# Up-projections with 512 moving columns: the low and high halves of the activations in one matmul, added at the eviction

## What is computed

```python
# gated net (four of them, ffn0 to ffn3), hidden width 2816
y = (silu(h @ w_gate) * (h @ w_up)) @ w_down
# net with a convolution (two of them, ffn4 and ffn5)
def conv_ffn(h, w_up, cw, cb, w_down):
    gu = causal_dwconv(h @ w_up, cw, cb)
    g, u = jnp.split(gu, 2, axis=-1)
    return (jax.nn.gelu(g, approximate=True) * u) @ w_down
```

## Time and profile before

| what | value |
|---|---|
| median of 3 runs | 1914.26 us (1911.96 to 1915.06) |
| the profiled execution's own time | 1912.59 us |
| its span | 1910.8 us |
| mean granted TensorE clock | 0.982 |
| PE busy | 1820.1 us (95%) in 11714 matmuls |
| DVE busy | 1409.9 us (74%) in 2264 instructions |
| ACT busy | 950.9 us (50%) in 1382 instructions |
| read from HBM | 379.90 MB, 199 GB/s over the span |

### The profile page before, as it was taken

How to read it: one execution, slowest core, us unless ns; L and a number is a source line. 1 busy time by engine, 2 the same in 40 slices (tenths; PEclk the granted TensorE clock), 3 DMA queues, 4 the chain that set the end, 5 groups by cost and what they waited for, 6 DMA issues and landing times.

```text
span 1910.8 us, 31883 instructions
## 1 busy us (share of the span) xinstructions
PE 1820.1 (95%) x11714; PEld 1619.5 (85%) x11714; DVE 1409.9 (74%) x2264; ACT 950.9 (50%) x1382; POOL 129.5 (7%) x170
## 2 busy tenths in 40 slices
PE   6999899899999999999999999999889998979998
PEld 5998677699989997788878799978689987769996
DVE  7778888687778778868665565558778866877884
ACT  5444465454435443555454454445664435664443
POOL 1001010000010000000000000000012200002210
PEclk9999999899999999999999999999999999999999
DMA  9878666357788777455530255554254554324453
GB/s 384 339 272 312 231 234 214 126 212 275 279 290 297 267 278 269 163 176 177 191 137 1 82 224 184 189 183 181 70 194 179 177 197 154 111 88 176 176 186 122
DMA packets 63782, 382.11 MB, mean 200 GB/s; under 512 B 7153, under 2 KB 7409, under 8 KB 27586
## 3 DMA queue, kind: packets, MB, share of 16 engines
q1 hardware_dynamic: 42912, 300.96, 43.8%
q0 software_dynamic: 20208, 78.79, 11.4%
q10 hardware_dynamic: 578, 1.22, 0.2%
HBM read 379.90 MB, written 1.05 MB: 199 GB/s over the span
## 4 chain that ended last, share of the span: by engine, by line
PE 86%; DVE 7%; ACT 4%; issue 1%; DMA 1%; SPq 1%; DVEq 0%; ACTq 0%
PE ps L540 13%; PE ps L541 13%; PE ps L542 13%; PE ps L475 11%; PE ps L477 11%; PE ps L476 11%; PE ps L561 1%; PE ps L810 1%; PE ps L563 1%; PE ps L562 1%; DVE ring_lo L1543 1%; PE ps L588 1%; PE ps L836 1%; PE ps L823 1%; DMA ring<-in_stream 1%
## 5 line engine op out<-in xcount | busy, mean ns | idle before, releaser
L1543 DVE TENSOR_TENSOR ring_lo<-ring,w_hi 128x1024 fp32r<-128x1024 f32 x534 | 647.5, 1223 | 330.5 <-ACT w_hi L1104 325.8
L1104 ACT ACTIVATE w_hi<-ring 128x1024 fp32r<-128x1024 f32 x556 | 583.8, 1057 | 596.8 <-PE ps L542 295.4
L540 PE MATMUL ps<-h_lo,w_hi 128*128 128x256 f32 x2064 | 585.2, 284 | 3.5 <-DVE h_lo L1611 2.6
L542 PE MATMUL ps<-h_hi,ring_lo 128*128 128x256 f32 x2064 | 584.8, 283 | 0.0
L541 PE MATMUL ps<-h_hi,w_hi 128*128 128x256 f32 x2064 | 584.7, 283 | 0.0
L540 PEld LDWEIGHTS ps<-h_lo,w_hi 128*128 128x128 f32 x2064 | 396.9, 192 | 4.3 <-issue 3.1
L541 PEld LDWEIGHTS ps<-h_hi,w_hi 128*128 128x128 f32 x2064 | 396.9, 192 | 0.0
L542 PEld LDWEIGHTS ps<-h_hi,ring_lo 128*128 128x128 f32 x2064 | 396.9, 192 | 0.0
L475 PE MATMUL ps<-w_hi,h_lo 128*128 128x512 f32 x580 | 235.3, 406 | 11.8 <-DVE h_lo L2009 6.4
L477 PE MATMUL ps<-w_hi,h_hi 128*128 128x512 f32 x580 | 228.5, 394 | 0.0
L476 PE MATMUL ps<-ring_lo,h_hi 128*128 128x512 f32 x580 | 228.2, 393 | 0.0
(11 more groups left out here) (352 smaller groups left out, 2016.2 us busy)
## 6 DMA issues: line engine op xcount, KB each, us to landing
ring<-in_stream SPq DMA_DIRECT2D x276, 1024.0 KB, 4.8
arena<-in_mod POOLq DMA_DIRECT2D x128, 512.0 KB, 5.7
arena<-in_mod SPq DMA_DIRECT2D x14, 512.0 KB, 13.4
gate<-in_wide POOLq DMA_DIRECT2D x3, 1536.0 KB, 10.3
arena<-in_nsaw POOLq DMA_DIRECT2D x2, 1072.0 KB, 9.0
ring<-in_stream SPq DMA_DIRECT2D x4, 512.0 KB, 14.8
arena<-in_konst POOLq DMA_DIRECT2D x1, 1295.5 KB, 8.9
arena<-in_mixw POOLq DMA_DIRECT2D x2, 576.0 KB, 9.9
```

The lines of the kernel that those rows point to most:

```text
L540: nc.tensor.matmul(dst, hi, x_lo, start=(r == 0 and i == 0 and b % 2 == 0), stop=False)
L542: mm = nc.tensor.matmul(dst, lo, x_hi, start=False, stop=(r == 3 and i == 1 and b % 2 == 1))
L1104: nc.scalar.activation(w_hi[:, q % SPLITS, :], ring[:, half % SLOTS, (q % 2) * QUARTER:(q % 2 + 1) * QUARTER], ACT.Copy).then_inc(w_hi_rea ...
L1543: v.tensor_tensor(ring_lo[:, slot, cs], ring[:, slot, cs], w_hi[:, q % SPLITS, :], ALU.subtract).then_inc(w_lo_ready, 1)
```

## The change

- The steps of all up-projections but the first of each gated net go through `up_wide`. `h_lo` and `h_hi` lie side by side (`h_both`), and the stationary w_hi block meets both in one matmul of 512 columns, in two pieces of 256; w_lo meets h_hi in a matmul of 256 columns that accumulates in the upper half. A block of output columns has a PSUM bank of its own: columns 0 to 255 hold the product with h_lo, columns 256 to 511 the others. A step takes four banks (`WIDE_BANKS`), two steps all eight.
- The halves are added at the eviction. ACT copies the low halves of two banks at a time to `wa` (two copies a step), DVE adds the high halves from PSUM to them in place (two additions a step). In a gated net Silu and the multiplication then read `wa`; the low part of the step before moves ahead of the multiplication.
- In a convolution net PE waits for the additions alone (`whole_ready`). The scaled copy with its bias moves from DVE to ACT (`taps`, four for a step), and the multiply-adds read `wa` and not PSUM. The second lag waits for the first as before, the first waits for ACT. DVE's order is: the additions, two splits (one of them POOL's), the convolution of all four blocks, a split, `join`, a split. At the end of the net the last step's convolution is interleaved with the first splits of the down-projection in another way.
- In a convolution net the first step too is wide, so it waits for h_lo of the first piece. `norm_at` puts the first pieces of these norms in banks 6 and 7, and PE waits for the second piece's h_lo before bank 7.
- In the prologue the first reciprocal stands after the sixth sum, the second after the eighth, and the first columns come ahead of the fifth sum. In ffn0's first step both units of the modulation stand behind all the splits.

```diff
+WIDE_BANKS = ((0, 1, 6, 7), (2, 3, 4, 5))
...
-        h_lo = over("h_lo", slab_at["hT"], [P, KC, T], F32R)
-        h_hi = over("h_hi", slab_at["h_hi"], [P, KC, T], F32R)
+        h_both = over("h_both", slab_at["hT"], [P, 2, KC, T], F32R)
+        h_lo, h_hi = h_both[:, 0, :, :], h_both[:, 1, :, :]
...
+            def up_wide(q, banks, it, per, fresh=None):
+
+                for r in range(4):
+                    low_part(q + r, it, per)
+                    slot, half, buf = ((q + r) // 2) % SLOTS, ((q + r) % 2) * QUARTER, (q + r) % SPLITS
+                    for i in range(2):
+                        if fresh is not None:
+                            pe.wait_ge(norm_lo, fresh + 2 * r + i + 1)
+                        for b in range(4):
+                            if fresh is not None and (r, i, b) == (0, 0, 3):
+                                pe.wait_ge(norm_lo, fresh + 2)
+                            o = i * 512 + b * P
+                            hi, lo = w_hi[:, buf, o:o + P], ring_lo[:, slot, half + o:half + o + P]
+                            nc.tensor.matmul(ps[:, banks[b], :].rearrange("p (w t) -> p w t", w=2), hi, h_both[:, :, 2 * r + i, :],
+                                             start=(r == 0 and i == 0), stop=False)
+                            mm = nc.tensor.matmul(ps[:, banks[b], T:2 * T], lo, h_hi[:, 2 * r + i, :], start=False, stop=(r == 3 and i == 1))
+                    mm.then_inc(quarter_done, 1)
...
+                    if conv:
+                        if v0 + j >= RING or it is not None:
+                            pe.wait_ge(whole_ready, val(it, GATED + 2 * (v0 + j - RING + 1), 2 * RING))
+                        up_wide(q0 + 4 * j, WIDE_BANKS[j % 2], it, TURNQ, 8 * m if j == 0 else None)
+                        return
...
+                    if j > 0:
+                        up_wide(q0 + 4 * j, WIDE_BANKS[j % 2], it, TURNQ)
+                    else:
+                        up_turned(q0 + 4 * j, UP_BANKS[j % 2], it, TURNQ, 8 * m)
```

ACT in a gated net:

```diff
+                    for n, b in enumerate(WIDE_BANKS[j % 2][::2]):
+                        low = ps[:, b:b + 2, 0:T]
+                        nc.scalar.activation(wa[:, n * 512:(n + 1) * 512].rearrange("p (b t) -> p b t", b=2), low, ACT.Copy).then_inc(low_kept, 1)
+                    keep_hi(f, j - 1, it)
+                    act.wait_ge(whole_ready, val(it, (UPS - 1) * f + j))
+                    nc.scalar.activation(wa[:, 0:512], wa[:, 0:512], ACT.Silu).then_inc(silu_ready, 1)
```

ACT in a convolution net:

```diff
+                    if j > 0:
+                        keep_low(j - 1, it)
                     split(q, q + 2, it, TURNQ)
                     if j > 0:
+                        taps(j - 1, it, 0)
+                        taps(j - 1, it, 1)
+                    split(q + 2, q + 3, it, TURNQ)
+                    if j > 0:
                         gelu(j - 1, it)
-                    split(q + 2, q + 4, it, TURNQ)
+                    split(q + 3, q + 4, it, TURNQ)
```

DVE in the prologue:

```diff
                 first_sums(0, 4)
-                first_roots()
                 dve.wait_ge(cols_in, 16)
                 first_cols(0)
-                first_sums(4, 8)
+                first_sums(4, 6)
+                first_root(0)
+                first_sums(6, 8)
+                first_root(1)
```

DVE in a gated net:

```diff
+                    for n, b in enumerate(WIDE_BANKS[j % 2][::2]):
+                        dve.wait_ge(low_kept, val(it, 2 * ((UPS - 1) * f + j - 1) + n + 1, 2 * turn))
+                        low = wa[:, n * 512:(n + 1) * 512].rearrange("p (b t) -> p b t", b=2)
+                        ins = v.tensor_tensor(low, ps[:, b:b + 2, T:2 * T], low, ALU.add)
...
+                    keep(j - 1, it)
                     dve.wait_ge(silu_ready, val(it, u + 1, turn))
+                    v.tensor_tensor(wb[:, half:half + 512], wa[:, 512:1024], wa[:, 0:512], ALU.mult).then_inc(h_ready, 1)
```

DVE in a convolution net:

```diff
-                        tick.mark(v.tensor_scalar(acc[:, c, :], src(c, 0), w, bias, ALU.mult, ALU.add))
+                    dve.wait_ge(conv_tap, val(it, 2 * (v0 + j) + pair[0] // 2 + 1, 2 * RING))
...
-                    split(q, q + 1, it, TURNQ)
+                    if j > 0:
+                        whole(j - 1, it)
+                    split(q, q + 2, it, TURNQ)
                     if j > 0:
                         conv(j - 1, it, (0, 1))
-                    split(q + 1, q + 2, it, TURNQ)
-                    if j > 0:
                         conv(j - 1, it, (2, 3))
```

More of the change, by code:

```diff
@@ L1223, in ffn_conv, with keep_low, taps @@
             def ffn_conv(f):
-                q0, v0 = BASE[f"ffn{f}"], UPS * (f - 4)
+                q0, v0, l = BASE[f"ffn{f}"], UPS * (f - 4), f - 4
+                def keep_low(j, it):
+                    act.wait_ge(quarter_done, val(it, q0 + 4 * j + 4, TURNQ))
+                    if v0 + j > 0 or it is not None:
+                        act.wait_ge(fconv_ready, val(it, v0 + j))
+                    for n, b in enumerate(WIDE_BANKS[j % 2][::2]):
+                        nc.scalar.activation(wa[:, n * 512:(n + 1) * 512].rearrange("p (b t) -> p b t", b=2), ps[:, b:b + 2, 0:T],
+                                             ACT.Copy).then_inc(low_kept, 1)
+                def taps(j, it, n):
+                    y = v0 + j
+                    act.wait_ge(whole_ready, val(it, GATED + 2 * y + n + 1, 2 * RING))
+                    if y > 0 or it is not None:
+                        if n == 0:
+                            act.wait_ge(gelu_ready, val(it, y))
+                        else:
+                            act.wait_ge(hid_ready_all, val(it, UPS * f + j))
+                    for c in (2 * n, 2 * n + 1):
+                        o = n * FC + c % 2 + 2 * j
+                        w = cols[:, bass.ds(val(it, COLS["fc_w"] + (l * 3 + 2) * 44 + o, 2 * RING), 1)]
+                        bias = cols[:, bass.ds(val(it, COLS["fc_b"] + l * 44 + o, 2 * RING), 1)]
+                        ins = nc.scalar.activation(wb[:, c * T:(c + 1) * T], wa[:, c * T:(c + 1) * T], ACT.Identity, bias=bias, scale=w)
+                    ins.then_inc(conv_tap, 1)
                 def gelu(j, it):
@@ L1242, in ffn_conv @@
                         step(PEEL + r, it)
+                keep_low(UPS - 1, None)
+                taps(UPS - 1, None, 0)
+                taps(UPS - 1, None, 1)
+                split(q0 + UPQ + 4, q0 + UPQ + 5)
                 gelu(UPS - 1, None)
-                split(q0 + UPQ + 4, q0 + UPQ + DOWNQ + LEAD - 2)
+                split(q0 + UPQ + 5, q0 + UPQ + DOWNQ + LEAD - 2)
             def qkv(q0, z0, w0, bufs, groups):
@@ L1589, in first_sums, with first_root @@
                     tick.mark(mod_col(n, mod_first[n], modraw[:, at:at + 1]))
-            def first_roots():
-                for tt in range(NT):
-                    dve.wait_ge(ms_ready, tt + 1)
-                    v.reciprocal(rstd[:, tt:tt + 1], rms[:, tt:tt + 1]).then_inc(rstd_ready, 1)
+            def first_root(tt):
+                dve.wait_ge(ms_ready, tt + 1)
+                v.reciprocal(rstd[:, tt:tt + 1], rms[:, tt:tt + 1]).then_inc(rstd_ready, 1)
             def first_cols(r):
@@ L1754, in step @@
                         split(max(q0 + 4 * j + LEAD + r, 4), q0 + 4 * j + LEAD + r + 1, it, 4 * turn)
-                        if mod and r % 2 == 1:
+                        if f == 0 and j == 0:
+                            if r == 3:
+                                mod_nth(t0)
+                                mod_nth(t0 + 1)
+                        elif mod and r % 2 == 1:
                             t = t0 + MOD_UP * j + r // 2
@@ L1869, in ffn_conv @@
                 d0 = q0 + UPQ
+                whole(UPS - 1, None)
                 conv(UPS - 1, None, (0, 1))
+                split(d0 + 4, d0 + 5)
                 conv(UPS - 1, None, (2, 3))
-                split(d0 + 4, d0 + 5)
+                split(d0 + 5, d0 + 6)
                 join(UPS - 1, None)
-                split(d0 + 5, d0 + DOWNQ + LEAD - 2)
+                split(d0 + 6, d0 + DOWNQ + LEAD - 2)
             def angles(w):
```

56 lines of the change are left out of this document (33 added, 23 removed).

## The result

The changed kernel takes 1903.34 us (median of 5 runs, 1899.39 to 1906.05) beside 1914.26 (1911.96 to 1915.34) for the kernel before: a ratio of 0.9944 [0.9934, 0.9955]. It is faster by 10.9 us or 0.6%, where 25 us were forecast, and lies outside the range. Its profiled execution took 1903.34 us, span 1901.7.

A forecast was written before the change was run, and what follows sets the result against it. PE, busy for 95% of the span, was taken as the bound. 1912.6 (profiled) - 26.4 + 0 + 0 + 0 + 1.2 = 1887.4 us; with the median 1.7 above, forecast 1889 us, range 1884 to 1898.

The forecast's parts named there:

- The wide matmul: Up-projections: a block goes from 360 to 347 ns, 13.3 ns saved in each of 1984 blocks, -26.4 us.
- a bound of zero saving: Wide blocks: if the operand's second piece costs as much as a further start, nothing is saved (0 us).
- first rival: Wide block saves only 2.5 ns or nothing, its moving operand being in two pieces: 1910.5 us, or 1915.5; chance 0.07.
- DVE in a gated step: Gated up-projections: two additions raise DVE's work from 8.9 to 10.2 of 11.09 us a step; cost 0.
- 1.2 of slack: Gated step: DVE keeps 1.2 us of slack where its waits were 2.7 us a step.
- DVE as the bound: Rival: DVE bounds the 30 steps with modulation; at 11.3 us a step 6 us are given back, 1895; chance 0.09.
- the handshakes in series: Rival, convolution step: ACT and DVE wait on each other in full, step 13.0 us, total 1931 us; chance 0.06.
- A convolution step: Convolution nets: DVE loses four scaled copies, gains two additions; ACT gains two copies and four taps; cost 0.
- The banks' 11.1: Convolution step: PE needs the banks at 11.1 us of the next step, counted as freed since 5.3.
- The prologue: Start of the kernel: later reciprocals make PE start at 25, not 22.77; net +1.2 us, between 0 and +3.
- Starts of the convolution nets: PE must have h_lo of the first piece; 0 for both nets, at most 0.5 us each.
- No table load: Sign, ffn4's loop: no table load stands there; Identity and Gelu needing different tables would bring about the 1931 us case.

The follow-up runs named there:

- groups of four: Changed kernel, with four matmuls of 512 columns and then four of 256 in each chunk of the wide steps: 1901.26 us, 0.9929.
- of eight: Changed kernel, with a quarter's eight matmuls of 512 columns ahead of its eight of 256: 1896.1 us, 0.9905.
- the best kernel: Changed kernel with eight-matmul groups of equal width, old prologue reciprocals, new order at the convolution nets' end, no POOL subtractions: 1892.61 us, 0.9891.
- the pause: Changed kernel, with PE waiting for its own last matmul after the first step of each gated net: 1905.81 us, 0.9955.

## Why the prediction was wrong

**The wide matmul** is the step that failed: its cost was mis-sized in the gated nets. The term was 1984 x 13.3 = 26.4 us. For the 704 blocks of the convolution nets it held: 9.1 us won, of 9.4. For the 1280 of the gated nets it was half: 6.6 ns each, 8.4 us won, of 17.0. I added two prices that had each been read from an unbroken stream of one width, 120 and 227 ns, and took it that they stay when the widths alternate. I had written that no row shows the two widths mixed, and had put a bound of zero saving on it, but as the reason for it I gave the operand in two pieces, at a chance of 0.07. The operand in one piece showed the same times, so that reason was wrong; groups of four and of eight made all nets alike, at prices that depend on the grouping, so the change of width is shown as the place of the cost, though not its mechanism. What came was between my forecast and that rival, and no rival of mine lay there. A range to 1898 excluded it; a saving of 5 to 13.3 ns would have reached 1905.

The 2.5 ns of that first rival as the whole price of a start did not come out either: 1910.5, with a measured 1903.3.

**DVE in a gated step**: 0, right. PE has no gap in ffn2's wide steps, and DVE still waits 1.61 us in a step, where 1.2 of slack were counted. From its timeline in the changed kernel:

```profile
646.03 1.23 DVE L1615 TENSOR_TENSOR ring_lo<-ring,w_hi 128x1024 fp32r<-128x1024 f32 x1 [1.61 <-ACT w_hi L1137]
647.18 1.22 DVE L1652 CUSTOM_DVE_ANT_0 arena<-arena 128x1024 f32<-128x1024 f32 x1
648.48 1.29 DVE L1847 TENSOR_TENSOR wa<-ps,wa 128x512 f32<-128x512 f32 x2
```

The additions follow the unit of the modulation without a wait for ACT's copies, as counted. Two rivals fell with this, DVE as the bound and the handshakes in series.

**A convolution step**: 0 for PE within the steps, right, but for a worse reason. I had DVE wait 1.1 us for the taps; past the first steps of a net it doesn't wait at all, because its own work fills the step: in 16 of 22 steps one subtraction stands behind POOL's and takes 1.4 us more. That the multiply-adds cost the same from SBUF as from PSUM was right (median 473 ns in both); that no other engine would be in their way was not, in four steps. The additions begin 6.6 us into the step and end at 7.8; I had them end at 5.3. The start-to-start figures that I took as the earlier trace rows (0.65, 0.45 and 0.39 us) aren't in those rows, which give means and sums; eight multiply-adds in 3.23 us bear out the 0.39. The banks' 11.1 gave PE that room. **Where it ends** I had costed nothing, without a reason: on the last step DVE is behind, by POOL's subtraction too, the down-projection wants splits sooner than an up-projection, and PE lost 2.3 us in the two nets. I had read the turned order at the end of the net and not counted it. It took both, the order and POOL: either edit alone ended the waits.

**The prologue**: +1.2, right as a net term. The first h_lo was to come at 23.5 and PE to start at 25. The timeline of the changed kernel, DVE and PE:

```profile
23.66 0.42 DVE L1682 TENSOR_TENSOR h_both<-hT,h_both 128x256 fp32r<-128x256 f32 x1 [2.94 <-ACT h_both L1186]
...
25.28 0.39 PE L532 MATMUL ps<-h_both,ring_lo 128*128 128x256 f32 x1 [2.41 <-DVE ring_lo L1615]
```

The reciprocals ran at 17.69 and 20.25, counted at 17.5 and 20.2. The units of the modulation gave back 1.2 us and not 0.9. **Starts of the convolution nets**: 0, right. No table load stood in the loops of these nets, although ACT does Identity and Gelu in turn there; each net has one load, ahead of its first Gelu (1424.5 us in ffn4), as before the change.

**What no step had**: 4.7 us outside the up-projections, of which up to 4.4 in stretches at 1.2 GHz. The program is the same there. I read this from the records of the granted clock of one execution; no run tested it, and its cause stays open.

The sum in measured terms: -8.4 (gated), -9.1 (convolution), +1.3 (prologue: 2.5 late at PE's start, 1.2 back in ffn0), +2.3 (down-projections' starts) make -13.9. The last matmul stood 9.2 us earlier, which leaves +4.7 for the rest. So of the miss the wide matmul makes 8.9 us (26.4 less 17.5), the down-projections' starts 2.3, the prologue 0.1 and the open rest 4.7, 16.0 in all; 1.7 of it is offset because I set the median 1.7 above the profiled execution, and here they are equal.

## What to carry to other kernels

A price read from an unbroken stream of one kind holds for such a stream; where a change mixes two kinds, keep the unmixed price and the worst one as two cases with a real chance each, and group equal widths before you trust either. Where an edit changes the order or the source memory of a full engine's work, look at what then runs beside its helpers: before, POOL's subtractions fell beside work from PSUM; after, beside work from SBUF, and the help turned into a hindrance. Read the distances of starts over a whole stage: that is what told the two paces apart here. The spread of the runs grew too (1899.4 to 1906.1 us, 1912.0 to 1915.3 before), but the patterns alone don't explain it: with groups of four, which have none, the runs lie 5.1 us apart.

## What was not expected of the hardware

- **Alternating widths have two steady paces.** Pairs of 512 and 256 columns start 346.7 ns apart on the mean (evenly, or in 3 of 12 stages 350 and 343 in turn) or 350, 350, 361, and stay so for the 320 or more pairs of a net. The slow one came in 26 of 26 stages entered on an unbroken stream of 256s, the quick one in 11 of 14 convolution nets entered behind a pause, and in 1 of 4 gated nets with a pause put in. What in PE makes a change of width cost, and what picks the pattern behind a pause (the 14 also began at 1.2 GHz), stays open.
- **DVE waits for POOL where both read SBUF.** A subtraction with two SBUF operands that starts while POOL subtracts took 2.62 us and up to 3.07, 1.22 without POOL, and a multiply-add from SBUF up to 2.40, 0.47 without; the additions with one operand in PSUM took 1.28 us for two beside the same POOL operation. The Trainium skill (SBUF — State Buffer, section "Who interferes with whom") says that a DVE instruction with two SBUF inputs contends with a GpSimd instruction that reads SBUF, while one with at most one SBUF input, outside the two-port modes, does not, and that whoever comes second waits for the whole of the other. The trace agrees: the subtraction ended 1.08 us after POOL's in all 16 cases, whether it had started 0.43 or 0.87 us behind it.
- **The clock's share varies from execution to execution.** PE was busy for 56.4 us at 1.2 GHz before, 65.3 after and 58.1 in the best kernel; over all kept traces it was 41.2 (the operand in one piece) to 75.6 (the pause). Runs of one kernel differ as well: with the operand in one piece 1899.2 us came at a mean granted clock of 0.987 and 1906.8 at 0.979.
